# A decoder trunk on one core: the mLSTM's denominators as a 129th column of its values, and new orders of steps in the mLSTM and in the latent attention

## Chip, cores, metric

One Trainium2 chip, one core. The metric is the device time of one launch in microseconds (us); each kernel is run several times and the median is compared. TensorE (PE) does the matrix products, VectorE (DVE) and ScalarE (ACT) the elementwise work, GpSimd (POOL) small vectors, SyncE (SP) issues the loads of the weights.

## What is computed

A trunk of 4 layers on 256 tokens of width 1024, all in float32. Each layer adds half a SwiGLU (hidden width 2816), then a mixer, then half a second SwiGLU, each of an RMS-normalised input; a last RMSNorm follows. The mixers are, in order, stick-breaking attention, mLSTM, latent attention, and stick-breaking attention again. The change touches the second and the third. Of the mLSTM (8 heads, values of 128, queries and keys of 64) this matters, written for all 256 tokens at once as the kernel does it:

```python
qk, v, o_pre, gates = split(x @ w_in)                    # 1024, 1024, 1024 and 16 columns
q, k = split(silu(causal_depthwise_conv(qk, conv_w)))
s   = (q @ k.T) * weights(gates)                         # causal, per head
num = s @ v                                              # (256, 128) per head
den = sum(s, axis=-1)                                    # (256,) per head
h   = num / maximum(abs(den), exp(-m))[..., None]
out = (sigmoid(o_pre) * rmsnorm(h, head_gain)) @ w_out
```

The latent attention projects to a query latent of 384 and a key/value latent of 256 (and a rotary key of 32), RMS-normalises both latents, projects them up for 16 heads, does causal softmax attention, and projects out.

## The kernel before

**Weights.** The weights are cut into pieces of at most 128 x 2048 numbers, numbered through the whole trunk. A piece goes through a ring of three slots: SP loads it into `raw` (L453), ACT writes its high part `whi` (rounded to fp32r, times the norm's gain; L472 with a gain, L468 and L463 without), DVE writes the rest `wlo` (L491, L487, L482). PE then makes each product from three passes, high by high, low by high and high by low (`passes`, L527; `turned_block`, L1599). ACT converts piece n when PE has used piece n - 3 (`piece_used`) and the load is in; DVE follows on `hi_ready`; PE waits for `lo_ready`. The activations stand as `xT_hi` and `xT_lo`, made by transposes on PE (`fill_pe`, L558; `y_fill`, L904), a copy by ACT (`split_act`, L549) and a subtraction by DVE (`split_dve`, L553).

**Order.** There is no planner: for each mixer four functions write out the steps of PE, ACT, DVE and POOL in a fixed order, and each engine works its own list in that order. A step that waits holds all that stands behind it on its engine. Between two sublayers `last_piece` and `first_piece` (PE), `norm_act` (ACT) and `norm_dve` (DVE) do the residual, the transposes of the residual stream and its sums of squares (L602). `norm_act` works four groups: the copy of each (L549), and behind groups 2 and 3 the squares of one half of the tokens.

**mLSTM** (`ml_pe`, `ml_act`, `ml_dve`). Pieces 0 and 2 to 12 are the projections (six blocks of 512 columns, two pieces each), piece 1 the gates, 13 to 16 the output projection (`out_piece`, four groups of 6 matmuls each). Blocks 1 to 5 share PSUM banks 4 and 5, so block b + 1 starts only when `evacuate` (L935) or `output_gate` (L1358) has emptied each bank (`proj_read`). Block 0 and 1 go to `stage`, are transposed (`transposes`, L894) and convolved (`convolve`, L1426, L1428). For each of two groups of 4 heads PE writes the logarithms of the weights (`log_weights`, L1270, L1273) and the scores (L950), DVE multiplies them (`weigh`, L1440), and `numerators` makes the numerators and denominators; `outputs` (DVE, L1450) divides. Then ACT sums squares (`squares`, L1366), POOL takes the root, DVE multiplies by root and gate (`gated`, L1463), and `y_fill` / `y_split` bring the result into `xT`.

In `numerators` each head and token tile has a product of 128 columns and, with the same weights loaded again, one of a single column of ones:

```python
for n, (w, kt) in enumerate(parts):
    pe.matmul(psum[:, 6 + t, hh * P:(hh + 1) * P], w, mv[:, kt, c:c + P], ...)                        # L1295
for n, (w, kt) in enumerate(parts):
    i = pe.matmul(psum[:, 3, t * GROUP + hh:t * GROUP + hh + 1], w, ones[:, 0:1], ...)                 # L1298
```

There are 12 products of each kind for a group (one for each head of tile 0, two for each of tile 1).

**Latent attention** (`lt_pe`, `lt_act`, `lt_dve`). `latents_0`, `latents_1` make the latents; `stats` (L1581) sums their squares with 10 products by one column of ones; POOL makes the roots and a diagonal, which `spread_row` (L1587) turns into a row. `k_rope_rows` (L1592, L1593) turns the rotary key; ACT copies it (L1744) and spreads it by two DMAs (L1747), then converts piece 5. `queries(g)` (L1599) runs in two halves of 18 matmuls, into banks 4 and 7; DVE empties them (L1885, `lq_read`), and each half of `queries(1)` waits for that. Pieces 11 to 14 are the output projection. Softmax of the last two groups of heads runs beside it: `scores`, `maxima` (DVE, L1900), `exps` (ACT, L1773), `normalise` (DVE, L1912), `transposes_p` (PE, L1671), `copy_p` (ACT, L1784), `values` (PE, L1686), `y_split`.

## Time and profile before

| what | us |
|---|---|
| median of 3 runs (lowest, highest) | 1965.38 (1963.99, 1965.87) |
| the profiled execution: its time | 1964.83 |
| the profiled execution: its span | 1963.1 |
| busy in the span: PE, PE's weight load, DVE, ACT, POOL | 1937.1, 1672.2, 1367.5, 1129.2, 64.4 |

The span runs from the first to the last instruction of the profile; 1.7 us of the execution's time lie around it. All times of rows are from the span's start. The mLSTM takes some 120 us of it (685 to 808), the latent attention some 100 (1180 to 1283); the rest is the SwiGLUs and the stick-breaking attention. Matmuls overlap in the pipeline, so the duration of one is longer than what it adds: that is the distance between starts. The profile shows a float32 matmul (neither operand fp32r) as two records.

### The profile page before, as it was taken

The numbers are of one execution on the slowest core, as the hardware profiler recorded it, in microseconds if no ns is written. First come the engines' busy times: TensorE is split into PE (matmuls) and PEld (weight loads), VectorE is DVE, ScalarE is ACT, GpSimd is POOL, SyncE is SP. The second block draws the span as 40 slices with busy tenths as digits, with TensorE's granted clock in tenths as the row PEclk, the third lists the DMA queues.
The fourth block names the chain that finished last, engine by engine and source line by source line (L and its number), as shares of the span: only waits on it lengthen the run. The fifth ranks groups of instructions, "written<-read, shape, count | busy, mean of one in ns | idle before, by whom it ended". The sixth has DMA issues, their size and how long they took to land.

```text
span 1963.1 us, 29566 instructions
## 1 busy us (share of the span) xinstructions
PE 1937.1 (99%) x10788; PEld 1672.2 (85%) x10802; DVE 1367.5 (70%) x1838; ACT 1129.2 (58%) x1678; POOL 64.4 (3%) x139
## 2 busy tenths in 40 slices
PE   8999999999999999999999999999999999999998
PEld 6888988888888878888888889888888888878887
DVE  6766676767777785676777666676677766767666
ACT  6555565555655565555565555665555556556553
POOL 2000000000100000000010001000000000000000
PEclk9999999999999999999999999999999999999999
DMA  6555534556555453465555554355555555535553
GB/s 218 193 191 192 172 129 145 198 192 197 176 193 187 162 179 129 129 214 191 187 165 192 190 180 131 112 193 192 192 172 187 187 189 180 178 110 170 192 192 118
DMA packets 244095, 343.35 MB, mean 175 GB/s; under 512 B 12077, under 2 KB 196026, under 8 KB 244026
## 3 DMA queue, kind: packets, MB, share of 16 engines
q1 hardware_dynamic: 242016, 340.29, 52.2%
q10 hardware_dynamic: 2010, 2.12, 0.4%
q8 instruction: 46, 0.75, 0.2%
q14 instruction: 23, 0.19, 0.0%
HBM read 340.27 MB, written 1.05 MB: 174 GB/s over the span
## 4 chain that ended last, share of the span: by engine, by line
PE 95%; DVE 2%; ACT 1%; DMA 1%; issue 0%; SPq 0%; POOL 0%; POOLq 0%; ACTq 0%
PE psum L688 33%; PE psum L527 33%; PE psum L696 17%; PE psum L985 5%; PE psum L1599 1%; PE psum L558 1%; DVE wlo L491 1%; PE psum L950 1%; ACT whi L472 1%; PE psum L1027 1%; PE psum L1046 1%; PE psum L960 0%; PE psum L1656 0%; PE psum L1295 0%; DMA raw<-in_ffn_wi 0%
## 5 line engine op out<-in xcount | busy, mean ns | idle before, releaser
L472 ACT ACTIVATE whi<-raw,gains 128x512 fp32r<-128x512 f32 (+2 forms) x876 | 557.0, 709 | 270.1 <-PE psum L696 197.9
L688 PE MATMUL psum<-xT,whi 128*128 128x512 f32 x2816 | 679.4, 393 | 1.6 <-DVE wlo L511 1.6
L491 DVE SCALAR_TENSOR_TENSOR wlo<-raw,gains,whi 128x512 fp32r<-128x512 f32 (+2 forms) x876 | 595.8, 742 | 58.1 <-ACT whi L472 57.9
L688 PEld LDWEIGHTS psum<-xT,whi 128*128 128x128 f32 x2816 | 523.1, 189 | 110.7 <-issue 4.2
L696 PEld LDWEIGHTS psum<-xT,wlo 128*128 128x128 f32 x2816 | 349.5, 192 | 6.9
L696 PE MATMUL psum<-xT,wlo 128*128 128x256 f32 x2816 | 351.9, 283 | 0.0
L804 DVE TENSOR_TENSOR gate_in_T<-psum,low 128x512 f32<-128x512 f32 x88 | 60.8, 691 | 342.2 <-ACT low L751 341.5
L487 DVE TENSOR_TENSOR wlo<-raw,whi 128x2048 fp32r<-128x2048 f32 x100 | 228.5, 2285 | 43.8 <-ACT whi L468 43.8
L527 PE MATMUL psum<-whi,hidT_lo 128*128 128x512 f32 x640 | 249.0, 389 | 0.0
L527 PE MATMUL psum<-whi,hidT_hi 128*128 128x512 f32 x640 | 249.0, 389 | 0.0
L527 PE MATMUL psum<-wlo,hidT_hi 128*128 128x512 f32 x640 | 249.0, 389 | 0.0
L527 PE MATMUL psum<-whi,xT 128*128 128x512 f32 x704 | 230.6, 396 | 7.3 <-DVE xT L553 3.1
L468 ACT ACTIVATE whi<-raw 128x2048 fp32r<-128x2048 f32 x100 | 190.6, 1906 | 29.2 <-PE psum L696 25.3
L527 PEld LDWEIGHTS psum<-whi,xT 128*128 128x128 f32 x704 | 132.2, 188 | 37.9 <-DVE xT L553 4.0
L527 PEld LDWEIGHTS psum<-whi,hidT_hi 128*128 128x128 f32 x640 | 120.1, 188 | 25.0
L527 PEld LDWEIGHTS psum<-whi,hidT_lo 128*128 128x128 f32 x640 | 120.1, 188 | 25.0
L527 PEld LDWEIGHTS psum<-wlo,hidT_hi 128*128 128x128 f32 x640 | 120.1, 188 | 24.9
L527 PE MATMUL psum<-wlo,xT 128*128 128x512 f32 x352 | 137.2, 390 | 0.0
L766 ACT ACTIVATE hidT_hi<-hid 128x512 fp32r<-128x512 f32 x80 | 50.6, 633 | 142.6 <-PE psum L527 106.6
L759 ACT ACTIVATE silu<-gate_in_T 128x512 f32<-128x512 f32 x88 | 55.6, 632 | 106.8 <-DVE gate_in_T L806 106.7
L985 PE MATMUL psum<-xT,whi 128*128 128x256 f32 x576 | 107.3, 285 | 1.1 <-DVE mix L1145 1.1
L751 ACT ACTIVATE low<-psum 128x512 f32<-128x512 f32 x88 | 52.4, 595 | 90.2 <-PE psum L688 90.2
(231 smaller groups left out, 1565.2 us busy)
## 6 DMA issues: line engine op xcount, KB each, us to landing
raw<-in_ffn_wi SPq DMA_DIRECT2D x350, 512.0 KB, 4.6
raw<-in_ffn_wo SPq DMA_DIRECT2D x176, 512.0 KB, 4.4
raw<-in_sb_w_in SPq DMA_DIRECT2D x48, 512.0 KB, 4.4
raw<-in_ml_w_in SPq DMA_DIRECT2D x24, 512.0 KB, 4.6
raw<-in_sb_w_out SPq DMA_DIRECT2D x16, 512.0 KB, 4.2
raw<-in_ml_w_out SPq DMA_DIRECT2D x8, 512.0 KB, 4.1
raw<-in_mla_w_out SPq DMA_DIRECT2D x8, 512.0 KB, 4.3
raw<-in_mla_w_in SPq DMA_DIRECT2D x4, 512.0 KB, 4.2
```

The costliest lines, as they stand in the source:

```text
L468: act.activation(whi[:, slot, 0:w], raw[:, slot, 0:w], ACT.Copy).then_inc(hi_ready, 1)
L472: last = act.activation(whi[:, slot, r], raw[:, slot, r], ACT.Copy, scale=gain_col(p.gain + k))
L487: dve.tensor_tensor(wlo[:, slot, 0:w], raw[:, slot, 0:w], hi[:, 0:w], ALU.subtract).then_inc(lo_ready, 1)
L491: last = dve.scalar_tensor_tensor(wlo[:, slot, r], raw[:, slot, r], gain_col(p.gain + k), hi[:, r], op0=ALU.mult, op1=ALU.subtract)
L527: m = pe.matmul(dst, a, b[:, slot, cols], start=first and n == 0, stop=last and n == 2)
L688: i = pe.matmul(psum[:, 4 + blk, :], whi[:, slot, k * 2 * FC + blk * P:k * 2 * FC + (blk + 1) * P], xT[:, 4 * part + k, :, :].rearrange("p ...
L696: i = pe.matmul(psum[:, 4 + blk, 0:SEQ], wlo[:, slot, k * 2 * FC + blk * P:k * 2 * FC + (blk + 1) * P], xT_hi[:, 4 * part + k, :], start=F ...
L751: act.activation(low[:, 0, :, :], psum[:, 4:6, SEQ:2 * SEQ], ACT.Copy).then_inc(low_done, 1)
L759: act.activation(silu[:, :, :], gate_in_T[:, :, :], ACT.Silu).then_inc(silu_done, 1)
L766: act.activation(hidT(last)[0], hid[:, :, :], ACT.Copy).then_inc(hid_hi_done, 1)
L804: dve.tensor_tensor(gate_in_T[:, :, :], psum[:, 4:6, 0:SEQ], low[:, 0, :, :], ALU.add).then_inc(proj_read, 1)
L985: i = pe.matmul(dst, w[:, m % RING, c:c + P], v[:, k0 + k, :], start=k0 + k == 0 and a == 0 and blk == 0, stop=k0 + k == KD - 1 and a == 2 ...
```

## The change

Five things are done.

1. `mv` becomes (token tile, head, 129), with ones written once by POOL into column 128; `numerators` does one product of 129 columns for each pair; results stand three to a bank in banks 6, 7 and 3 (`unit`). `outputs` takes the magnitudes in two instructions and divides in four rather than two.
2. In `norm_act` ACT converts the mLSTM's piece 2 ahead of the first squares and of the copy of group 3.
3. On DVE the first half of `evac(1, stage)` goes ahead of `conv(6)`, and `evac(2, ...)` ahead of `convolve(1, (0, 1))`.
4. The first two `y_fill` of the mLSTM go ahead of piece 12, into banks 0 and 1, with their splits; the other two move to the end of `out_piece` 0 and 1.
5. In the latent attention the first half of `queries(0)` goes ahead of `stats`; piece 12 is converted ahead of `exps(2, 0)` (ACT) and of the second `y_split` (DVE); `scores(3)`, `values(2)`, `transposes_p(3)` and `values(3)` change places in the output pieces, and the third `y_split` goes behind `exps(3, 0)` and `maxima(3, 1)`.

```diff
@@ norm_act, behind norm_split(act, j, g)
+                if g == 2 and j and subs[j].kind == "ml":
+                    converts(act, convert_act, subs[j].piece0 + 2)
@@ numerators
-                            pe.matmul(psum[:, 6 + t, hh * P:(hh + 1) * P], w, mv[:, kt, c:c + P],
-                                      start=hh == 0 and n == 0, stop=n == t, skip_group_check=True)
-                        for n, (w, kt) in enumerate(parts):
-                            i = pe.matmul(psum[:, 3, t * GROUP + hh:t * GROUP + hh + 1], w, ones[:, 0:1],
-                                          start=t == 0 and hh == 0 and n == 0, stop=n == t, skip_group_check=True)
+                            i = pe.matmul(psum[:, bank, c:c + P + 1], w, mv[:, kt, GROUP * g + hh, :], start=c == 0 and n == 0,
+                                          stop=n == t, skip_group_check=True)
@@ ml_pe, end
             numerators(1)
+            y_fill(pe, s, 0, 0)
+            y_fill(pe, s, 1, 1, False)
             piece(12)
+            pe.wait_ge(tr_read, s.norm_fill0 - 4 + 2)
             pe.wait_ge(num_read, 2)
-            y_fill(pe, s, 0, 6)
-            out_piece(pe, s, 0, {1: lambda: y_fill(pe, s, 1, 7)})
-            out_piece(pe, s, 1, {1: lambda: y_fill(pe, s, 2, 6)})
-            out_piece(pe, s, 2, {1: lambda: y_fill(pe, s, 3, 7)})
+            out_piece(pe, s, 0, {3: lambda: y_fill(pe, s, 2, 6)})
+            out_piece(pe, s, 1, {3: lambda: y_fill(pe, s, 3, 7)})
+            out_piece(pe, s, 2)
@@ ml_act
-            for n in (2, 3, 4, 5):
+            for n in (3, 4, 5):
...
             conv(14)
+            y_split(act, s, 0, 0)
+            y_split(act, s, 1, 1)
             squares(1)
             output_gate(1)
-            y_split(act, s, 0, 6)
             conv(15)
-            y_split(act, s, 1, 7)
             conv(16)
@@ ml_dve
+            evac(1, stage, (0,))
             conv(6)
-            evac(1, stage)
+            evac(1, stage, (1,))
...
             conv(8)
+            evac(2, mv[:, :, 0:GROUP, 0:P])
             convolve(1, (0, 1))
-            evac(2, mv[:, :, 0:NCOL])
...
             outputs(1)
-            y_split(dve, s, 0, 6)
+            y_split(dve, s, 0, 0)
+            y_split(dve, s, 1, 1)
             gated(1)
             conv(15)
-            y_split(dve, s, 1, 7)
@@ ml_set_up (POOL)
+            pool.memset(mv[:, :, :, P:P + 1], 1.0)
@@ lt_pe
             latents_1()
+            queries(0, (0,))
             stats()
             k_rope_rows()
-            queries(0)
+            queries(0, (1,))
             spread_row()
...
-            out_piece(pe, s, 1, {0: lambda: values(2), 1: lambda: scores(3)})
-            out_piece(pe, s, 2, {1: lambda: transposes_p(3)})
-            values(3)
+            out_piece(pe, s, 1, {0: lambda: scores(3), 1: lambda: values(2)})
+            out_piece(pe, s, 2, {0: lambda: transposes_p(3), 2: lambda: values(3)})
@@ lt_act
             copy_p(1)
+            conv(12)
             exps(2, 0)
             y_split(act, s, 1, LT_AV[1])
             exps(2, 1)
-            conv(12)
             copy_p(2)
-            y_split(act, s, 2, LT_AV[2])
             conv(13)
             exps(3, 0)
+            y_split(act, s, 2, LT_AV[2])
@@ lt_dve
             maxima(2, 1)
+            conv(12)
             y_split(dve, s, 1, LT_AV[1])
             normalise(2, 0)
             normalise(2, 1)
-            conv(12)
-            y_split(dve, s, 2, LT_AV[2])
             conv(13)
             maxima(3, 0)
             maxima(3, 1)
+            y_split(dve, s, 2, LT_AV[2])
```

## Rows read from the trace of the kernel before

**Rows 1.** The page: busy time, and the groups of the weights' conversions.

```profile
PE 1937.1 (99%) x10788; PEld 1672.2 (85%) x10802; DVE 1367.5 (70%) x1838; ACT 1129.2 (58%) x1678; POOL 64.4 (3%) x139
...
L491 DVE SCALAR_TENSOR_TENSOR wlo<-raw,gains,whi 128x512 fp32r<-128x512 f32 (+2 forms) x876 | 595.8, 742 | 58.1 <-ACT whi L472 57.9
...
L487 DVE TENSOR_TENSOR wlo<-raw,whi 128x2048 fp32r<-128x2048 f32 x100 | 228.5, 2285 | 43.8 <-ACT whi L468 43.8
...
L468 ACT ACTIVATE whi<-raw 128x2048 fp32r<-128x2048 f32 x100 | 190.6, 1906 | 29.2 <-PE psum L696 25.3
```

**Rows 2.** Waits of PE: who waited for whom, us in total, times, longest.

```profile
PE psum L527 <- DVE mix L935: 1.6, 2, 1.2
```

**Rows 3.** Groups of PE's instructions by line and shape: busy us, mean ns of one.

```profile
L1295 PE MATMUL psum<-mix 128*128 128x128 f32 x48 | 8.9, 298 | 0.0
...
L1298 PE MATMUL psum<-ones,mix 128*128 128x1 f32 x48 | 6.3, 223 | 0.0
...
L1270 PE MATMUL psum<-mix 128*128 128x256 f32 x16 | 3.8, 379 | 0.0
```

**Rows 4.** Timeline of PE in the mLSTM: start, us, engine, line, instructions, idle before.

```profile
695.77 0.28 PE L1233 MATMUL psum<-xT,whi 128*16 128x256 f32 x1
697.41 0.50 PE L527 MATMUL psum<-whi,xT 128*128 128x512 f32 x1 [1.36 <-DVE wlo L491]
...
717.07 0.47 PE L527 MATMUL psum<-whi,xT 128*128 128x512 f32 x1 [1.23 <-DVE mix L935]
...
753.18 0.69 PE L1295 MATMUL psum<-mix 128*128 128x128 f32 x4
...
754.08 0.69 PE L1295 MATMUL psum<-mix 128*128 128x128 f32 x4
...
785.84 0.50 PE L527 MATMUL psum<-whi,xT 128*128 128x512 f32 x1 [1.55 <-DVE xT L553]
```

**Rows 5.** Timeline of ACT where the mLSTM begins.

```profile
687.80 1.05 ACT L602 ACTIVATE y<-h 128x1024 f32<-128x1024 f32 x1
...
690.51 0.60 ACT L549 ACTIVATE xT<-psum 128x512 fp32r<-128x512 f32 x1 [1.56 <-PE psum L558]
...
692.04 7.45 ACT L472 ACTIVATE whi<-raw,gains 128x512 fp32r<-128x512 f32 x12
```

**Rows 6.** Timeline of DVE in the mLSTM.

```profile
691.14 0.69 DVE L553 TENSOR_TENSOR xT<-psum,xT 128x512 fp32r<-128x512 f32 x1 [1.34 <-ACT xT L549]
...
716.18 1.39 DVE L935 TENSOR_SCALAR mix<-psum,rstd 128x512 f32<-128x512 f32 x2
...
772.22 2.19 DVE L1463 SCALAR_TENSOR_TENSOR y<-y,mix 128x128 f32<-128x128 f32 x8
```

**Rows 7.** Timelines of PE, ACT and DVE where the latent attention begins.

```profile
1199.71 2.39 PE L1581 MATMUL psum<-ones,mix 128*128 128x1 f32 x20 [0.47 <-ACT mix L1733]
...
1209.19 0.47 PE L1599 MATMUL psum<-sp_hi,whi 128*128 128x256 f32 x1
...
1203.28 0.38 ACT L1744 ACTIVATE mix<-psum 64x256 f32<-64x256 f32 x1 [3.63 <-PE psum L1593]
...
1207.54 0.69 DVE L1885 TENSOR_TENSOR mix<-psum,mix 128x512 f32<-128x512 f32 x1
```

**Rows 8.** Stretches there: us, busy PE, PEld, DVE, ACT, POOL with counts, clock, DMA.

```profile
1203.00:1206.40 3.40, 3.40 (x16) 3.23 (x16) 0.07 (x1) 1.53 (x3) 2.12 (x5) 0.51 0.30 69
1206.40:1210.00 3.60, 3.60 (x31) 3.55 (x31) 2.53 (x5) 0.39 (x1) 0.00 (x0) 1.00 0.78 163
```

**Rows 9.** Timelines of PE, ACT and DVE in the latent attention's output pieces.

```profile
1257.25 0.47 PE L527 MATMUL psum<-whi,xT 128*128 128x512 f32 x1 [0.99 <-DVE wlo L487]
...
1277.87 0.50 PE L527 MATMUL psum<-whi,xT 128*128 128x512 f32 x1 [1.42 <-DVE xT L553]
...
1248.43 0.56 ACT L1773 ACTIVATE mix<-psum,mix 128x256 f32<-128x256 f32 x1 [2.76 <-DVE mix L1905]
...
1251.25 0.69 DVE L553 TENSOR_TENSOR xT<-psum,xT 128x512 fp32r<-128x512 f32 x1 [1.99 <-ACT xT L549]
```

More of the change, by code:

```diff
@@ L927, in out_piece, with evacuate @@
             i.then_inc(piece_used, 1)
[L929 to L931 removed]
+        def evacuate(dve, s, b, last, dst, tiles=(0, 1)):
+            for t in tiles:
                 block_wait(dve, s, b, t, last)
[L933 to L938 removed]
+                src = psum[:, pair(b)[t], 0:math.prod(dst.shape[2:])]
+                if len(dst.shape) == 4:
+                    src = src.rearrange("p (h n) -> p h n", h=dst.shape[2])
+                dve.tensor_scalar(dst[:, t], src, rstd[:, t:t + 1], None, ALU.mult).then_inc(proj_read, 1)
         def scores_pe(pe, g, bank, k_T, q, start):
@@ L1413, in conv, with evac @@
                 converts(dve, convert_dve, s.piece0 + n)
[L1415 to L1416 removed]
+            def evac(b, dst, tiles=(0, 1)):
+                evacuate(dve, s, b, 2 * b + 2, dst, tiles)
             def convolve(part, tiles):
@@ L1606, in queries @@
                 pe.wait_ge(c_lo_done, 2)
-                for b in range(2):
+                for b in halves:
                     if g:
```

47 lines of the change are left out of this document (24 added, 23 removed).

## The prediction

> **What bounds the kernel now.** The page comes first: PE is busy for 1937.1 of 1963.1 us, no other engine for more than 70% [rows 1]. So a change can win in two ways only: fewer or shorter matmuls, or less of the 26 us in which PE stands still. The waits of PE then say what those 26 us are made of; inside the two mixers each is a wait of 0.4 to 1.6 us for one late step of DVE or ACT, as the two for `evacuate` [rows 2]. The groups by shape price the matmuls that are removed [rows 3], and the timelines show who is late and by how much [rows 4 to 7, 9]. The stretches give TensorE's granted clock [rows 8]. I do not look at the DMA queues further: every load meant here is issued two pieces ahead, and in none of these waits is a load the releaser.
>
> **Part 1, the denominators.** Each group has 12 products of one column, which stand in the profile as 24 records, 48 in all [rows 3]. One head of token tile 1 has four records of 128 columns and four of one, and takes 754.08 - 753.18 = 0.90 us [rows 4], so 0.112 us a record. That a record of one column costs as much as one of 128 is seen on `stats`: 20 records of one column take 2.39 us, 0.12 each [rows 7]; what they pay is the load of their weights. Removed: 48 x 0.112 = 5.4 us, all of it on PE and so all of it on the path, if nothing else is late.
> The Trainium skill (TensorE: Matmul & The Clock Gate, Back-to-back issue gap) has a floor of some 25 ns from start to start for small matmuls that need no new weights. By that floor the 48 records would be worth 1.2 us, not 5.4; the rows above measure 0.12 us for pairs of load and matmul, and the measurement decides.
> Added: the remaining 48 records have 129 columns. The trace has none such. Below: as 128, 0.112 us, and a little less is excluded since more is streamed. Above: the 256-column float32 records of `log_weights`, 3.8 / 16 = 0.24 us [rows 3], which would add 48 x 0.125 = 6.0 us. 129 is next to 128, so I take 0.001 us a record, +0.05 in sum, and keep +6.0 for the range. The operand rows now begin at multiples of 516 bytes; nothing in the trace shows that, and it is the reason for keeping the upper end.
> DVE's `outputs` has one more magnitude and two more divisions, of the same elements in all: some 0.4 us for each group, twice. Behind the first call stand `conv(12)` and a wait for scores that idles DVE by several us, so it costs nothing. Behind the second stand the two splits that open the output projection (part 4). POOL, busy 64.4 us in all [rows 1], does its one memset in the idle time ahead of the mLSTM. `evac` writes runs of 128 rather than of 512; its source is PSUM in both cases, at 0.69 us for each tile [rows 6], and I cost it at nothing.
>
> **Part 2, piece 2 of the mLSTM.** After the gates PE waits until 697.41 for the low part of piece 2, 1.36 us of idle [rows 4], since ACT begins its high part only at 692.04 [rows 5]. Moved ahead of the squares it begins at 687.8, takes a third of 7.45, 2.5 us, and ends at 690.4. ACT then has the squares (1.1, to 691.5) and the copy of group 3 (0.6, to 692.1), which ran at 690.51 before [rows 5]; DVE's split of it, 691.14 before, is at 692.2 to 692.9 [rows 6]. PE needs that for the gates, which it reaches at 693.1: 0.2 us to spare. DVE makes the low part by 692.9 + 4 x 0.742 less overlap, 695.6 [rows 1]; PE comes for it at 695.9, 0.3 us to spare. I take the whole 1.36. If the margins fail, by a slot or a load coming later than I think, the wait only moves in front of the gates: 0.3 is left of the gain. Next in line is the load of piece 5, which hangs on the low part of piece 2 and moves with it.
>
> **Part 3, the evacuations.** PE waits 1.23 us until 717.07, because `evac(1, stage)` stands behind `conv(6)` and runs at 716.18 [rows 4, 6]. With its first tile ahead of `conv(6)`, PE can go on at once; its second tile is wanted only by `transposes(1)`, half a piece (2.7 us) later, and is there 1.5 us before that. Gained 1.23. `evac(2)` ahead of `convolve` takes away the other wait for that line, 1.6 - 1.2 = 0.4 us [rows 2]. `conv(6)` ends 0.7 later for it, and has a whole piece of PE time to spare.
>
> **Part 4, the first transposes of the result.** PE stands idle 1.55 us until 785.84 [rows 4]: it transposes the result when piece 12 is over and waits through copy and subtraction. The first group's result is ready at 772.22 + 2.19 = 774.4, before PE ends the second numerators [rows 6], so the two fills fit there, and piece 12 (5.4 us) covers the splits. In the shortened schedule I count: numerators over at 769.8, fills to 770.8, piece 12 to 776.3; DVE `conv(14)` to 771.9, `outputs(1)` at 2.3 to 774.2, splits to 775.5. That is 0.8 us to spare, and the 1.55 goes. Who is late next: the third and fourth splits stand behind `conv(16)` and `conv(17)`, and those start when PE has used pieces 13 and 14. `y_fill(3)` finds the third split done some 0.6 us before it, and `out_piece(3)` waits some 0.1 us, as it did before.
>
> Sum of the mLSTM: 5.4 - 0.05 + 1.36 + 1.23 + 0.4 + 1.55 = 9.9 us.
>
> **Part 5a, the statistics.** PE waits 0.47 us for ACT's squares ahead of `stats` [rows 7]. Half of `queries(0)`, 18 x 0.116 = 2.1 us [rows 8], put ahead of it hides that. But `stats` and `k_rope_rows` end 2.1 - 0.47 = 1.65 us later, and a chain hangs on them: the rotary key is done when ACT copies it at 1203.28, ACT then issues two DMAs and only then converts piece 5, DVE follows and then empties `queries(0)` at 1207.54 to 1208.2 [rows 7], which `queries(1)` waits for. So that release comes 4.9 us behind the copy: at 1208.2 before, when PE came at 1209.19 [rows 7] and saw no wait, and at 1208.2 + 1.65 = 1209.9 now. PE itself will be there at about 1207.4, and stand for 2.5 us. Why did it come so late before? In 1203.00 to 1206.40 the granted clock was 0.51, the 1.2 GHz level, right after the wait and the one-column products: 16 records in 3.40 us, against 31 in 3.60 behind it [rows 8]. That cost 16 x (0.21 - 0.116) = 1.5 us, and this loss now falls into a wait. In sum the latent attention goes on at 1209.9 and not at 1209.2: **0.7 us lost**. Bounds: 0.9 gained at most if the chain were shorter than I read (PE cannot be released before its old 1208.2 plus what `stats` moved); 2.4 lost if the clock falls again in or before the new wait and slows what follows.
>
> **Part 5b, the output pieces.** PE waits 0.99 us for the low part of piece 12 and 1.42 us for the last split [rows 9]. Piece 12 on ACT (1.91 [rows 1]) fits into its idle 2.76 us ahead of `exps(2, 0)`, and on DVE (2.29 [rows 1]) into the 1.99 us ahead of the second split [rows 9]: 0.2 us over, and `normalise(2, 0)` and `transposes_p(2)` move by no more than that, with the score work behind not binding. With `values(3)` one group (1.36 us) before the end of piece 13, its copy and subtraction (0.6 + 0.7 and gaps) are just hidden. Gained: 0.99 + 1.42 = 2.4, less 0.1.
>
> **Sum.** 9.9 - 0.7 + 2.3 = 11.5 us from the profiled execution's 1964.83: **1953.3**. The median of the runs is 0.55 above that execution; I leave that in the range. The idle times of the rows leave out some 0.1 us at each wait, because a matmul's duration overlaps the next start (697.41 - 695.77 = 1.64 for an idle of 1.36 [rows 4]), so six waits may give 0.6 more.
>
> **Rivals.**
> (A) The forecast, chance 0.62.
> (B) The clock falls in the new wait ahead of `queries(1)`, or `k_rope_rows` falls into the slow stretch. For it: the one slow stretch of this trace lies just behind stall and one-column products [rows 8], and the new stall is longer than any in the mixers. Against: the waits of 1.2 to 1.6 us in the mLSTM left the clock at its upper level. Price 1.5 us again: 1954.8. Chance 0.14. The Trainium skill (TensorE: Matmul & The Clock Gate, The HAM clock gate) says that an idle array falls back to half clock and that steady work brings it back; by that, the trace agrees for the old stall, and (B) would be the outcome here.
> (C) One of the margins of 0.1 to 0.3 us in parts 2, 4 or 5b is not there, and a wait comes back in another place. Price 1 to 2 us: about 1955. Chance 0.12.
> (D) The 129th column is dear, as a second pass over the operand or as a row that begins out of line: between 0.112 and 0.24 us a record, up to +6.0: 1956 to 1959.3. For it: nothing measured. Against: the change is by one column. Chance 0.07.
> (E) The other side. The same mechanism, worse: a record of 129 columns from rows of 516 bytes costs over 0.112 + (11.5 + 3.9) / 48 = 0.43 us, so that `numerators` alone gives back more than the change brings; it decides from 0.35 us on. For that each record would take four times its present one. At 0.45: 1953.3 + 48 x 0.34 = 1969.6. Chance 0.03.
> (F) The products of one column were nearly free beside the others, so that removing them brings little: then part 1 gives 1 rather than 5.4, and 1957.7. Against it stands the even 0.112 and 0.12 of part 1. Chance 0.02.
>
> **Range and chances.** 1951.5 takes in the 0.6 of the idle times, a median like the lowest run, and a chain in 5a that costs nothing; 1957.5 takes in (B) with (C), the higher median, and the lower half of (D). About 0.2% of the time, 3.9 us, is what a measurement of this kernel tells from no change: below 1961.5 is faster. (A), (B), (C), (F) and nearly all of (D) lie there: faster 0.95, same 0.02, slower 0.03.
>
> **What would show it.** In the changed profile: L1298's records gone, those of `numerators` at 0.11 apart and 48 in number; no wait of PE for L491 behind the gates and none for `evacuate`; no wait between piece 12 and the first output piece; a new wait of about 2.5 us of PE on L1599 for DVE's L1885, the surest mark of 5a; waits for L487 and for the last split of the latent attention gone or below 0.2. The first output product of the mLSTM's piece 16 some 10 us earlier than before, that of the latent attention 11 to 12. I am wrong in the large if the distance between records of 129 columns is not 0.11 us, and in the small if a wait of over 0.5 us stands anywhere else in the two mixers.

## The result and the profile after

| | median us | lowest, highest | ratio to before, 95% interval |
|---|---|---|---|
| before, 4 runs | 1964.85 | 1963.99, 1965.87 | |
| changed, 4 runs | 1952.98 | 1952.00, 1953.34 | 0.9937 (0.9925 to 0.9949) |

The change makes the kernel faster by 11.9 us, 0.6%; the forecast was 1953.3, which is 11.5 us below the profiled execution of before and 11.55 below this median. The profiled execution of the changed kernel took 1952.87 us, with a span of 1951.1.

The busy times, from the page of the changed kernel:

```profile
PE 1929.9 (99%) x10740; PEld 1666.6 (85%) x10754; DVE 1368.4 (70%) x1844; ACT 1129.1 (58%) x1678; POOL 64.6 (3%) x140
```

PE has 48 instructions fewer than in [rows 1] and is busy for 7.2 us less; DVE has its six more (the division of `outputs` in four pieces and the magnitudes in two, for two groups). Idle time of PE in the span fell from 26.0 to 21.2 us. The waits of PE in the changed kernel (waited for, us in total, times, longest) name the larger part of these 21.2 us:

```profile
PE psum L2188 <- DMA mix<-in_ln_ffn: 5.5, 1, 5.5
PE psum L1614 <- DVE mix L1900: 2.4, 1, 2.4
...
PE psum L691 <- DVE gate_in_T L807: 0.4, 1, 0.4
PE psum L528 <- DVE xT L554: 0.2, 1, 0.2
```

The wait for the evacuation [rows 2] is not among them; those for piece 2, for the last splits and for piece 12 of the latent attention [rows 4, 9] are gone too. L1614 (`turned_block`, that is `queries(1)`) for L1900 (DVE's evacuation of `queries(0)`) is new. The first row is the start of the kernel and was there before.

To say where the time went, I take distances between two starts of PE, which no overlap of durations disturbs. Four of them are used from here on: the mLSTM (from the first transpose ahead of it to the first transpose behind it), and in the latent attention from its first transpose to the start of `queries(1)` (a), from there to the first score (b), and from there to the first transpose of the next sublayer (c).

| us | mLSTM | a | b | c |
|---|---|---|---|---|
| before | 124.08 | 31.29 | 7.67 | 65.23 |
| changed | 113.21 | 31.79 | 9.09 | 62.44 |
| difference | -10.87 | +0.50 | +1.42 | -2.79 |
| forecast | -9.9 (-10.5 with the overlaps) | +0.7 | 0 | -2.3 |

Both profiles lack one record where the first score is found: the group there has two records with 0.29 us of idle time before it, in others three records with none. So are those of `e2b`, `e5`, `e8` and `e9` below. In these six, b is 0.2 us too long and c 0.2 too short. Where kernels of both kinds are compared, I count to the record behind that group, which stands in all: so counted, b is 8.10 us before and 9.51 in the changed kernel, and c 64.80 and 62.02.

The rest of the difference lies elsewhere. The first transpose of the mLSTM comes 0.55 us earlier, ahead of all that the change touches. All of it arises in the first 20 us of the kernel, some 0.1 by the wait for the first loads and the rest in the first products behind it. This start differs from run to run: in the fourteen profiles of this study that transpose stands between 682.98 and 684.82 us, so two single runs can differ by up to 1.8 us for this alone. Behind the latent attention 0.3 us are lost, mostly in the new row above for L807. The same wait of 0.37 us stands in `e5` and `e11`, whose latent attention is as before, so the new orders did not bring it; its cause is open.

**The numerators.** Groups by shape, and PE's timeline (start, us, line, instructions), of the changed kernel:

```profile
L1303 PE MATMUL psum<-mix 128*128 128x129 f32 x48 | 5.7, 274 | 0.0
```

```profile
765.94 2.84 PE L1303 MATMUL psum<-mix 128*128 128x129 f32 x24
768.62 1.04 PE L907 MATMUL psum<-ident,y 128*128 128x128 f32 x8
...
792.62 0.50 PE L528 MATMUL psum<-whi,xT 128*128 128x512 f32 x1 [0.19 <-DVE xT L554]
```

24 records of 129 columns take 768.62 - 765.94 = 2.68 us: 0.112 each, the same as a record of 128 columns in [rows 4]. The 129th column, and rows that begin at multiples of 516 bytes, cost nothing that can be read here. Right behind stand the two early fills, and between piece 12 and the output projection there is no wait; the 0.19 at 792.62 is the fourth split, where the prediction had 0.1 and the trace of before 0.16.

**Pieces and evacuations.** ACT's and DVE's timelines of the changed kernel:

```profile
687.24 2.55 ACT L473 ACTIVATE whi<-raw,gains 128x512 fp32r<-128x512 f32 x4
```

```profile
691.35 0.69 DVE L554 TENSOR_TENSOR xT<-psum,xT 128x512 fp32r<-128x512 f32 x1 [2.11 <-ACT xT L550]
691.96 2.73 DVE L492 SCALAR_TENSOR_TENSOR wlo<-raw,gains,whi 128x512 fp32r<-128x512 f32 x4
...
710.96 0.75 DVE L939 TENSOR_SCALAR mix<-psum,rstd 128x512 f32<-128x512 f32 x1
```

Piece 2 is converted by ACT at 687.24 to 689.8 (forecast 687.8 to 690.4, in a trace that runs 0.55 later), its low part ends at 694.7, and PE comes for it at 695.3 without a wait. The first tile of `evac(1)` now stands at 710.96, ahead of the low part of piece 6.

**The latent attention.** PE's timeline where it begins, and the release chain on ACT and DVE:

```profile
1189.74 2.29 PE L1596 MATMUL psum<-ones,mix 128*128 128x1 f32 x20
...
1198.22 0.35 PE L1614 MATMUL psum<-sp_hi,whi 128*128 128x256 f32 x1 [2.39 <-DVE mix L1900]
```

```profile
1193.12 0.38 ACT L1759 ACTIVATE mix<-psum 64x256 f32<-64x256 f32 x1 [4.92 <-PE psum L1608]
1193.53 1.36 ACTq L1762 DMA_DIRECT2D mix<-mix  x2
1194.99 1.15 ACT L464 ACTIVATE whi<-raw 128x512 fp32r<-128x512 f32 x2 [1.49 <-issue]
```

```profile
1196.17 1.29 DVE L483 TENSOR_TENSOR wlo<-raw,whi 128x512 fp32r<-128x512 f32 x2 [3.89 <-ACT whi L464]
1197.39 1.28 DVE L1900 TENSOR_TENSOR mix<-psum,mix 128x512 f32<-128x512 f32 x2
```

`stats` has no wait ahead of it any more, where before it had 0.47 [rows 7]. In the order of time: the rotary key is copied at 1193.12, ACT spends 1.36 us on issuing its two DMAs, then converts piece 5 for 1.15; DVE makes the low part, and only then empties the bank that `queries(1)` wants. PE stands for 2.39 us. The stretches of the changed kernel there (us, then busy PE, PEld, DVE, ACT, POOL, then granted clock and DMA) show what follows it:

```profile
1194.00:1195.60 1.60, 1.60 (x14) 1.43 (x13) 0.00 (x0) 0.61 (x2) 1.14 (x4) 1.00 0.33 76
1195.60:1198.10 2.50, 0.23 (x2) 0.00 (x0) 1.93 (x4) 0.93 (x3) 0.00 (x0) 1.00 0.77 164
1198.10:1201.50 3.40, 3.28 (x16) 3.31 (x17) 2.04 (x4) 1.67 (x3) 0.00 (x0) 0.55 0.79 164
```

In the 3.4 us behind the wait the granted clock is 0.55, near the 1.2 GHz level, and PE does 16 products where at the upper level it did 31 in 3.6 us [rows 8]. So the slow stretch of the trace before, which lay over `queries(0)`, is still there; it has moved behind the wait, over products that the end of the kernel hangs on.

### The profile page after: what moved, and what is told of

Its sections match the earlier page's. It is cut to its first block, busy times and chain, and to the rows that moved or that the text cites. A ratio compares the mean times of both kernels' runs of the same rounds, so it can differ in the third digit from the quotient of the medians.

```text
span 1951.1 us, 29477 instructions
## 1 busy us (share of the span) xinstructions
PE 1929.9 (99%) x10740; PEld 1666.6 (85%) x10754; DVE 1368.4 (70%) x1844; ACT 1129.1 (58%) x1678; POOL 64.6 (3%) x140
## 4 chain that ended last, share of the span: by engine, by line
PE 97%; DVE 1%; ACT 1%; DMA 0%; issue 0%; SPq 0%; ACTq 0%; POOL 0%; POOLq 0%; DVEq 0%
PE psum L528 35%; PE psum L691 33%; PE psum L699 17%; PE psum L986 5%; PE psum L1614 1%; PE psum L559 1%; PE psum L951 1%; PE psum L1028 1%; PE psum L1047 1%; PE psum L961 0%; DVE wlo L492 0%; ACT whi L473 0%; PE psum L1671 0%; DMA raw<-in_ffn_wi 0%; PE psum L1701 0%; PE psum L1578 0%
## 5 line engine op out<-in xcount | busy, mean ns | idle before, releaser
L807 DVE TENSOR_TENSOR gate_in_T<-psum,low 128x512 f32<-128x512 f32 x88 | 60.9, 692 | 341.6 <-ACT low L754 340.9
```

Source lines behind the costliest of these rows:

```text
L807: dve.tensor_tensor(gate_in_T[:, :, :], psum[:, 4:6, 0:SEQ], low[:, 0, :, :], ALU.add).then_inc(proj_read, 1)
```

## The experiments

Each is the changed kernel with one edit, but for `e5_column_alone` and `e11_column_and_y`, which start from the kernel before. Here are the results of all, with distances as in the table above (the kernel of `e2` was run once more as `e2b`). The kernel before was run anew beside them, with medians of 1964.59 to 1965.46, and the ratios are to those runs. Medians that lie less than 1 us apart are therefore better compared by these ratios.

| kernel | median us (lowest, highest; runs) | ratio to before (95%) | mLSTM | a | b | c |
|---|---|---|---|---|---|---|
| e1_old_stats | 1951.19 (1951.00, 1951.39; 4) | 0.9927 (0.9911 to 0.9944) | 113.22 | 31.30 | 7.46 | 62.47 |
| e2_queries_first | 1950.04 (1948.27, 1951.75; 4) | 0.9924 (0.9908 to 0.9941) | 113.17 | 29.05 | 7.45 | 62.64 |
| e2b_again | 1948.25 (1) | | 113.18 | 29.04 | 7.67 | 62.24 |
| e3_two_products | 1957.07 (1956.28, 1957.73; 4) | 0.9956 (0.9940 to 0.9973) | 118.43 | 31.78 | 7.34 | 62.48 |
| e4_old_output | 1955.24 (1954.74, 1955.65; 4) | 0.9948 (0.9932 to 0.9965) | 113.15 | 31.78 | 8.88 | 65.44 |
| e5_column_alone | 1963.58 (1961.26, 1964.53; 10) | 0.9988 (0.9978 to 0.9997) | 121.61 | 32.85 | 7.67 | 65.23 |
| e6_old_piece2 | 1953.28 (1952.59, 1955.35; 4) | 0.9941 (0.9924 to 0.9958) | 114.85 | 31.78 | 8.77 | 62.65 |
| e7_old_evac | 1953.45 (1952.81, 1954.67; 4) | 0.9942 (0.9925 to 0.9958) | 114.86 | 31.78 | 8.71 | 62.61 |
| e8_old_y | 1956.44 (1955.79, 1957.04; 4) | 0.9956 (0.9939 to 0.9972) | 118.22 | 31.78 | 7.40 | 62.25 |
| e9_split_stats | 1948.72 (1948.15, 1948.98; 4) | 0.9917 (0.9901 to 0.9934) | 113.20 | 29.14 | 7.67 | 62.45 |
| e10_filled_wait | 1952.13 (1951.30, 1954.10; 4) | 0.9940 (0.9923 to 0.9956) | 113.18 | 31.79 | 7.34 | 62.64 |
| e11_column_and_y | 1957.80 (1956.86, 1958.56; 6) | 0.9966 (0.9953 to 0.9978) | 116.82 | 31.30 | 7.45 | 65.25 |

### The statistics as before (part 5a undone)

```diff
             latents_1()
-            queries(0, (0,))
             stats()
             k_rope_rows()
-            queries(0, (1,))
+            queries(0)
```

> The changed kernel with all of queries(0) behind stats again, as it was. Theory 1 (the chain rotary key, ACT's copy and DMA issue, piece 5, DVE's evacuation releases queries(1), and moving stats only pushed it back): PE waits 0.5 us for the squares, the wait of 2.4 us on the first queries(1) shrinks to under 0.3, the way from the sublayer's first transpose to queries(1) falls from 31.8 to 31.3 us, and from there to the first scores from 9.1 to 7.7 us, since the slow clock falls on queries(0) where the chain hides it: 1.9 us faster than the changed kernel, some 1951.1. Theory 2 (the move was worth its 0.5 us and the loss behind it is the clock alone, which falls after the one-column products in either order): the slow stretch comes all the same behind queries(1), and the time is 0.5 us longer than the changed kernel's, 1953.5.

Measured: 1951.19, that is 1.8 us faster than the changed kernel. The way from the first transpose to the record behind the first score is 39.4 us against 41.3, 1.9 less. PE's timeline and the stretches of this kernel:

```profile
1188.73 2.39 PE L1596 MATMUL psum<-ones,mix 128*128 128x1 f32 x20 [0.47 <-ACT mix L1747]
```

```profile
1192.20:1195.60 3.40, 3.40 (x20) 3.40 (x21) 0.32 (x1) 1.53 (x3) 1.96 (x5) 0.63 0.36 82
1195.60:1198.00 2.40, 2.40 (x19) 2.40 (x19) 1.57 (x3) 0.00 (x0) 0.00 (x0) 0.81 0.77 155
```

The old wait of 0.47 is back, the one ahead of `queries(1)` is gone, and the slow clock lies over `queries(0)` again. It costs little there, since PE, if it were quicker, would only wait for the release chain. So part 5a as a whole is a loss: 0.5 for the chain, 1.4 for the clock, which now falls on work that counts.

### The evacuations of `queries(0)` ahead of piece 5 on DVE

```diff
@@ lt_dve
-            conv(5)
             queries(0, 0)
             queries(0, 1)
+            conv(5)
             c_kv_scaled()
```

> The changed kernel with DVE's two evacuations of queries(0) ahead of its part of piece 5. Theory 1: the wait of 2.4 us on queries(1) goes, and with it the slow stretch of the clock behind it (1.4 us): 3.8 us faster than the changed kernel, some 1949.2; the next in line is the scaled key/value latent, done 0.3 us before PE wants it. Theory 2 (the clock falls after the one-column products anyway): the wait goes, but a slow stretch of 1.5 us stays: 2.4 us faster, 1950.6.

Measured: 1950.04, with a = 29.05, 2.7 us less than in the changed kernel, and no wait ahead of `queries(1)`. That is the whole wait, and more by the 0.3 that durations hide: the bank was late only because its evacuation stood behind the low part of piece 5. The stretch of `stats` and the rotary key in this kernel:

```profile
1192.00:1195.20 3.20, 3.20 (x23) 2.79 (x23) 0.65 (x3) 0.83 (x2) 2.69 (x5) 1.00 0.13 31
```

The clock stays at 1.00 here. But the four times fall into two pairs, 1948.47 and 1948.27 against 1951.75 and 1951.62. I ran the same kernel once more to catch a long one:

> The kernel of e2_queries_first once more, for a second trace of it. Its four times fell into two pairs, near 1948.4 and near 1951.7. If the clock explains it (theory 2), a trace with the longer time shows a slow stretch behind stats or in queries(0) that now costs its full 1.5 us, as nothing hides it; a trace with the shorter time shows none.

It took 1948.25 and its trace is like the first. With the wait gone, PE still goes through `stats` and the 32-row products of the rotary key, behind which the clock fell in `e1` and in the kernel before; that it does so in some executions of `e2` could account for the 3.3 us of the two long runs. The start, which differs by up to 1.8 us, could be a part of it. Neither long run was profiled, so this stays open.

### Two products instead of one (part 1 undone on PE alone)

```diff
@@ numerators
-                            i = pe.matmul(psum[:, bank, c:c + P + 1], w, mv[:, kt, GROUP * g + hh, :], ...)
+                            pe.matmul(psum[:, bank, c:c + P], w, mv[:, kt, GROUP * g + hh, 0:P], ...)
+                        for n, (w, kt) in enumerate(parts):
+                            i = pe.matmul(psum[:, bank, c + P:c + P + 1], w, mv[:, kt, GROUP * g + hh, P:P + 1], start=False, ...)
```

> The changed kernel, but each product of 129 columns cut into one of 128 and one of the last column, with the weights loaded twice; same banks, same outputs step. If a record of one column costs as much as one of 128 (0.11 us, the weight load), 48 more records cost 5.4 us: 1958.4. If they are nearly free (25 to 40 ns), 1.2 to 1.9 us: 1954.5. If the orders of the change hang on the shorter numerators, up to 1 us of waits is added.

Measured: the mLSTM takes 118.43 us, 5.22 more, or 0.109 for each of the 48 records; the median is 4.1 us higher. The groups by shape of this kernel:

```profile
L1303 PE MATMUL psum<-mix 128*128 128x128 f32 x48 | 8.9, 298 | 0.0
L1306 PE MATMUL psum<-mix 128*128 128x1 f32 x48 | 6.3, 223 | 0.0
```

These are the two rows of [rows 3] again, with the operand now in rows of 129 numbers: neither stride nor place changes them. In the profiled execution the slow clock fell on `queries(0)`, as this stretch shows, and most of it was hidden: counted to the record behind the first score, b is 7.99 us and not 9.51.

```profile
1199.50:1202.60 3.10, 3.10 (x19) 3.10 (x20) 0.04 (x1) 1.53 (x3) 1.95 (x5) 0.67 0.32 73
```

That is why the median could move by less than 5.22; the other three runs have no profile.

### The column alone, on the kernel before

```diff
-                            pe.matmul(psum[:, 6 + t, hh * P:(hh + 1) * P], w, mv[:, kt, c:c + P], ...)
-                        for n, (w, kt) in enumerate(parts):
-                            i = pe.matmul(psum[:, 3, t * GROUP + hh:t * GROUP + hh + 1], w, ones[:, 0:1], ...)
+                            i = pe.matmul(psum[:, bank, c:c + P + 1], w, mv[:, kt, GROUP * g + hh, :], ...)
@@ and `unit`, `outputs`, `evac`, the memset of column 128, as in the change
```

> The kernel before with the 129th column alone, all orders as before. If the removed products are worth their record price and nothing else is late: 5.4 us less in the mLSTM (its way from the first transpose to that of the next sublayer 124.1 before, 118.7 here), 1959.8 in all, and the four waits of PE in the mLSTM (1.4, 1.2, 0.4, 1.6) stand as before. Rival: the orders of before hang on the longer numerators, and the last wait grows by up to 1 us.

Measured: the mLSTM takes 121.61 us, not 118.7. It is shorter by 2.47 us only, the median by 1.3 (by 1.9 against the runs of the kernel before beside it, 1965.46). The products did not get dearer. PE's, ACT's and DVE's timelines of this kernel behind piece 12:

```profile
777.62 0.60 PE L905 MATMUL psum<-ident,y 128*128 128x128 f32 x4
781.35 0.50 PE L528 MATMUL psum<-whi,xT 128*128 128x512 f32 x1 [3.13 <-DVE xT L554]
```

```profile
776.49 0.31 ACT L1369 ACTIVATE mix<-y 128x128 f32<-128x128 f32 x1 [4.58 <-DVE y L1458]
...
778.85 1.24 ACT L1361 ACTIVATE mix<-psum,rstd 128x512 f32<-128x512 f32 x2
779.99 0.58 ACT L550 ACTIVATE xT<-psum 128x512 fp32r<-128x512 f32 x1
```

```profile
771.94 2.48 DVE L492 SCALAR_TENSOR_TENSOR wlo<-raw,gains,whi 128x1024 fp32r<-128x1024 f32 x2 [0.89 <-ACT whi L473]
```

The 1.55 us of [rows 4] have become 3.13. PE comes to the first fill earlier, but ACT's copy of it stands behind `squares(1)` (eight of 0.29 us, 776.49 to 778.85) and `output_gate(1)` (1.24 us), those behind DVE's `outputs(1)`, and that behind the low part of piece 14, which ends at 774.3. This list did not get shorter with the numerators. The stretches of this kernel show the second cost:

```profile
778.00:781.00 3.00, 0.22 (x2) 0.00 (x0) 0.40 (x1) 3.00 (x11) 1.84 (x2) 1.00 0.34 120
781.00:784.40 3.40, 3.05 (x10) 2.42 (x11) 3.40 (x10) 1.65 (x2) 0.00 (x0) 0.73 0.00 0
784.40:788.00 3.60, 3.60 (x16) 2.92 (x15) 2.08 (x3) 0.60 (x1) 0.00 (x0) 0.78 0.30 64
```

Behind the wait of 3.1 us the clock falls in part of both stretches; behind the wait of 1.55 us in the same place of the kernel before it did not. In the latent attention a is 1.56 longer than before (32.85), since the slow stretch on `queries(0)` lasted longer in this execution; so of the 2.47 us only some 0.9 are left in the trace. And 0.3 of the 2.47 do not come from the column: PE's first wait for an evacuation is 0.85 us here and was 1.23, for a reason that the section on pieces 2 and 3 shows.

### The first fills as before (part 4 undone), and parts 1 and 4 together

```diff
@@ e8, ml_pe (ACT's and DVE's lists go back likewise)
             numerators(1)
-            y_fill(pe, s, 0, 0)
-            y_fill(pe, s, 1, 1, False)
             piece(12)
+            y_fill(pe, s, 0, 6)
...
@@ e11: the kernel before, with the column as in e5 and the lists of part 4 as in the change
```

> The changed kernel with the first two transposes of the mLSTM's result behind piece 12 again. The wait of 1.55 us comes back between the first of them and the output projection; 1.7 us by the distance of starts: 1954.7. Rival: numerators end 2.7 us sooner relative to the splits than before, so that DVE's squares and gates are late as well and more than 2 us come back.

> The kernel before with the 129th column and the early transposes of the result, nothing else. The column alone brought only 2.5 us in the mLSTM, since the wait behind piece 12 grew from 1.55 to 3.13 us and the clock fell behind it. Here that wait cannot stand: the mLSTM's way from the first transpose to the next sublayer's falls by 5.3 + 1.7 = 7.0 from 124.1 to 117.1 us, four and a half more than the column alone, and the total is 1958.3. If the growth of the wait had another cause, part of it comes back in another place, and the way is 118 or more.

Measured: without part 4 the mLSTM takes 118.22 us, 5.01 more than in the changed kernel, where the forecast had priced part 4 at 1.55 and the expectation above at 1.7. PE's timeline and the stretches of that kernel:

```profile
778.38 0.50 PE L528 MATMUL psum<-whi,xT 128*128 128x512 f32 x1 [3.12 <-DVE xT L554]
```

```profile
778.00:781.40 3.40, 3.02 (x10) 2.42 (x11) 3.40 (x10) 1.68 (x2) 0.00 (x0) 0.75 0.00 0
781.40:785.00 3.60, 3.60 (x16) 2.91 (x15) 2.11 (x3) 0.60 (x1) 0.00 (x0) 0.76 0.28 64
```

It is the wait of 3.1 us and the clock behind it, as in `e5`. Its median is only 3.5 us above the changed kernel; in the profiled execution the clock fell on `queries(0)` in the latent attention (b is 7.40 against 9.09, the record missing in both). Parts 1 and 4 on the kernel before bring 124.08 - 116.82 = 7.26 us. Their forecast terms were 5.4 and 1.55, in sum 6.9 with the 129th column; the rest, 0.3, has the size of the overlap at one wait. So these two terms are right together and wrong one by one: part 1 alone is worth 2.5, part 4 in its presence 4.8 (7.26 - 2.47) on the kernel before and 5.0 on the changed one.

### Piece 2, and the evacuations (parts 2 and 3 undone)

```diff
@@ e6: norm_act and ml_act
-                if g == 2 and j and subs[j].kind == "ml":
-                    converts(act, convert_act, subs[j].piece0 + 2)
-            for n in (3, 4, 5):
+            for n in (2, 3, 4, 5):
@@ e7: ml_dve
-            evac(1, stage, (0,))
             conv(6)
-            evac(1, stage, (1,))
+            evac(1, stage)
...
-            evac(2, mv[:, :, 0:GROUP, 0:P])
             convolve(1, (0, 1))
+            evac(2, mv[:, :, 0:GROUP, 0:P])
```

> The changed kernel with the conversion of the mLSTM's piece 2 behind the squares again. The wait of 1.4 us for its low part comes back, 1.5 us by the distance of starts, and the steps behind it move along: the mLSTM's way 113.2 becomes 114.7, the total 1954.4. Rival: the load of piece 5, which hangs on it, comes late and adds a wait of its own.

> The changed kernel with the two evacuations behind conv(6) and behind convolve again. The waits of 1.23 and 0.37 us come back, by the distance of starts 1.4 and 0.4; since piece 2 is earlier than in the kernel before, the first may be larger by up to 0.3 us. The mLSTM's way 113.2 becomes 115.0 to 115.3, the total 1954.9.

PE's timelines, first of the kernel with the old piece 2, then of the one with the old evacuations:

```profile
697.82 0.50 PE L528 MATMUL psum<-whi,xT 128*128 128x512 f32 x1 [1.38 <-DVE wlo L492]
```

```profile
714.73 0.47 PE L528 MATMUL psum<-whi,xT 128*128 128x512 f32 x1 [0.76 <-DVE mix L939]
```

Each wait is back in its place (beside the 0.76 also the one of 0.37 at 730.87), and each mLSTM is longer by 1.64 and 1.65 us. Part 2 is thus worth 1.64 (forecast 1.36) and part 3 1.65 (1.63). But the first wait for an evacuation is 0.76 us, where it was 1.23 before. ACT's timelines, of the kernel before and of the one with the old evacuations, show what set it:

```profile
703.70 2.56 ACT L472 ACTIVATE whi<-raw,gains 128x512 fp32r<-128x512 f32 x4 [4.20 <-DMA raw<-in_ml_w_in]
```

```profile
701.37 2.56 ACT L473 ACTIVATE whi<-raw,gains 128x512 fp32r<-128x512 f32 x4 [2.89 <-DMA raw<-in_ml_w_in]
```

This is piece 5, whose conversion starts when its load is in: 19.5 us behind the mLSTM's first transpose before, 17.4 here. DVE makes its low part next, and everything up to the evacuation follows without a gap in DVE's list. So with piece 2 early this load comes 2.1 us earlier, PE only 1.6, and the wait is shorter by the difference. In `e5` and `e11` the load came at 19.2 and 19.4, and the wait was 0.85 and 1.10.

Beside this the medians rise by only 0.30 and 0.47 us (by the ratios, 0.8 and 1.0). In both kernels the profiled execution is the longest of the four, by 1.7 and 1.0 us, and without it the others lie around 1953. Part of that is the start: the first transpose of the mLSTM comes 0.95 and 0.33 us later in these two profiles than in that of the changed kernel. An execution in which the clock does not fall behind the wait of `queries(1)` would be shorter too, but I have no profile of one. The distances decide for what a part saves; what the median moved by is not settled for these two.

### The output pieces as before (part 5b undone)

```diff
@@ lt_pe (ACT's and DVE's lists go back likewise)
-            out_piece(pe, s, 1, {0: lambda: scores(3), 1: lambda: values(2)})
-            out_piece(pe, s, 2, {0: lambda: transposes_p(3), 2: lambda: values(3)})
+            out_piece(pe, s, 1, {0: lambda: values(2), 1: lambda: scores(3)})
+            out_piece(pe, s, 2, {1: lambda: transposes_p(3)})
+            values(3)
```

> The changed kernel with the order of the latent attention's output pieces, conversions and splits as before. The two waits of PE, 1.0 for piece 12 and 1.4 us for the last split, come back as they were: 2.4 by the idle times, 2.8 by the distance between the first scores and the first transpose of the next sublayer (62.4 now, 65.2 before): 1955.8. Rival: DVE's and ACT's queues have moved so that only one of the two comes back: 1954.2.

The waits of PE in this kernel:

```profile
PE psum L1614 <- DVE mix L1901: 2.4, 1, 2.4
...
PE psum L528 <- DVE xT L554: 1.6, 2, 1.4
...
PE psum L528 <- DVE wlo L488: 1.0, 1, 1.0
```

Both waits of [rows 9] are back; counted from the record behind the first score, c is 64.79, 2.8 us more than in the changed kernel, and the median 2.3 more. The forecast had 2.4 - 0.1 for it. The difference is again what durations hide at two waits, and the 0.1 that I took off was not lost.

### Is it the wait that lets the clock fall?

```diff
@@ lt_pe
             spread_row()
+            pe.wait_ge(table_read, 2)
+            for _ in range(18):
+                pe.matmul(psum[:, 0, 0:SEQ], c_hi[:, 0, 0:P], c_hi[:, 0, :], start=True, stop=True)
             queries(1)
```

> The changed kernel with 18 products of 256 columns into a bank that is free, put ahead of queries(1), where PE waits 2.4 us; they compute nothing that is used. If it is the long wait that lets the clock fall behind it, 2.1 us of added work cost nothing and bring 1.4 us: from queries(1) to the first scores 7.6 us and not 9.1, no stretch below the upper level behind queries(1), 1951.5 in all. If the one-column products bring the fall, it comes as before and the time is the changed kernel's 1953.0 or a little more.

PE's timeline and the stretches of this kernel:

```profile
1195.44 2.49 PE L1717 MATMUL psum<-sp_hi 128*128 128x256 f32 x18
1198.18 0.36 PE L1614 MATMUL psum<-sp_hi,whi 128*128 128x256 f32 x1 [0.24 <-DVE mix L1903]
```

```profile
1195.50:1198.10 2.60, 2.44 (x20) 2.20 (x18) 1.96 (x4) 0.99 (x3) 0.00 (x0) 1.00 0.78 165
1198.10:1201.50 3.40, 3.32 (x28) 3.35 (x29) 2.70 (x6) 1.68 (x3) 0.00 (x0) 1.00 0.79 168
```

`queries(1)` starts as late as before (a = 31.79), held by the same release, but 18 products whose result nobody reads fill the time ahead of it. The clock stays at 1.00, 28 products run in the 3.4 us that held 16, and b, counted to the record behind the first score, falls from 9.51 to 7.99 us. In this profile filling the time kept the clock up, so it is the engine's standing still that made it fall in this place; the 1.5 us are its price. This rests on one profile against four with the wait (the changed kernel, `e4`, `e6`, `e7`), in each of which the clock fell behind it. The profiled run took 1951.30, the other three 1952.42, 1951.84 and 1954.10: the median is only 0.85 below the changed kernel, and by the ratios to the kernel before (0.9940 against 0.9937) nothing is gained. The times of whole runs thus do not show the effect; only the trace does.

### A version that avoids both

```diff
@@ lt_pe, with DVE's list as in e2
+                    if c:                                   # in latents_1, behind the rotary half
+                        pe.wait_ge(c_hi_done, 2)
+                        stat_products(lambda k: k < 4)      # 16 of the 20 records
...
             latents_1()
-            queries(0, (0,))
-            stats()
             k_rope_rows()
-            queries(0, (1,))
+            stats()                                         # the products for k == 4 alone
+            queries(0)
```

> The changed kernel with DVE's evacuations of queries(0) ahead of piece 5, and with stats cut in two: the 8 products whose squares are ready stand between the two halves of the second latent piece, the rotary key next, which covers the wait for the last squares, then the last 2 products and all of queries(0). Theory 1 (a release chain from the rotary key) and theory 2 (the clock falls behind a stretch of one-column products) agree that no wait is left: 29.1 us from the first transpose to queries(1). They differ in the clock: if one-column products and the 32-row products in one piece bring the fall, it should be gone here in every execution, and the runs should lie together at 1949, where e2_queries_first spread over 1948.3 to 1951.8.

PE's timeline and the stretches of this kernel:

```profile
1184.06 1.84 PE L1590 MATMUL psum<-ones,mix 128*128 128x1 f32 x16
...
1188.79 0.69 PE L1615 MATMUL psum<-mix 32*128 32x256 f32 x2
...
1189.85 0.61 PE L1590 MATMUL psum<-ones,mix 128*128 128x1 f32 x4
```

```profile
1184.00:1188.00 4.00, 4.00 (x37) 4.00 (x36) 2.41 (x3) 0.00 (x0) 0.00 (x0) 1.00 0.13 36
1188.00:1192.00 4.00, 4.00 (x30) 3.47 (x29) 0.23 (x2) 0.94 (x3) 1.10 (x2) 1.00 0.49 152
1192.00:1196.00 4.00, 4.00 (x34) 3.95 (x33) 1.85 (x3) 1.36 (x3) 1.58 (x4) 1.00 0.78 162
```

Most of the one-column products are done while the second half of the latents is still to come, the rotary key goes ahead of the last four, and there is neither a wait nor an unbroken row of 20 small products. The clock is 1.00 throughout. The median is 1948.72, 4.3 us below the changed kernel (3.9 by the ratios) and 16 below the one before, the four runs within 0.8 us of each other: the lowest median of several runs. Its fast runs are no faster than those of `e2` (1948.3); what it adds is that no run near 1951.7 came. Four runs are few for that, and whether breaking up the row did it is not shown.

## Why the prediction was right

**Part 1, the numerators: right in its sum, under a condition that only part 4 met.** Each of the 48 one-column records cost 0.109 (`e3`), 0.112 was forecast, and the 129th column costs nothing. But "all of it on PE and so all of it on the path, if nothing else is late" passes over the point: without part 4 something is late at once. Alone, more than half of the 5.4 us went into a longer wait behind piece 12 and into the clock (`e5`). Rivals D, E and F are excluded: the products were neither dear with 129 columns nor nearly free with one. The floor of 25 ns of the Trainium skill (TensorE: Matmul & The Clock Gate, Back-to-back issue gap), named in the prediction, would have made these records worth 1.2 us; `e3` says 5.22. The prediction had it for products that need no new weights, and every one of these records loads its own.

**Parts 2 and 3: right.** 1.64 and 1.65 us against 1.36 and 1.63. Both margins of part 2 held: the low part of piece 2 is there 0.6 us before PE comes (forecast 0.3). The term of part 2 was too small by what the idle column leaves out, as the prediction had said of it. That of part 3 is right partly by luck: the idle column leaves out 0.5 us at its two waits, and the first wait was 0.5 us shorter once piece 2 was early. The prediction had said that in none of these waits a load is the releaser. That is so one step back, but the chain of DVE and ACT ahead of the evacuation began with the load of piece 5.

**Part 4: right in place, too small for what it does.** The step "the 1.55 goes" took the wait from the trace of before, and that wait was to grow with part 1. Worked out on the shortened schedule, as the margins were, it would have been 3.1 us with a slow clock behind it. The error does not show in the total, since part 1 was credited with what belongs to part 4: 7.26 measured for both. The spare time before the first output product was 0.8 us, as forecast (DVE's splits end at 774.1; piece 12 begins at 769.4 and takes 5.6, so PE comes at 775.0).

**Part 5a: the mechanism right, its price off by the clock.** The new wait was forecast at 2.5 us and measured 2.39, at the instruction and for the release that the prediction named; with its chain from the copy of the rotary key to the evacuation, 5.1 us from 1193.12 to 1198.2, where 4.9 was read. The cost up to `queries(1)` was 0.5 us (0.7 forecast). What failed is the end of its sum, "this loss now falls into a wait". The slow clock of [rows 8] did leave `queries(0)`, but did not vanish into the wait: it began behind it and cost 1.4 us more (b = 9.09 against 7.67). That is rival B, at about the price of 1.5 that it had been given: the forecast counted it as the less likely case (0.14). I had held against it that the waits of 1.2 to 1.6 us in the mLSTM left the clock alone; the new wait was longer than any of them, and `e5` and `e8` show that one of 3.1 us in the mLSTM does have a slow stretch behind it. The rule of the Trainium skill (TensorE: Matmul & The Clock Gate, The HAM clock gate), that an idle array falls back to half clock, led to the right outcome here, and `e10` agrees: with the idle time filled, the clock stayed up. The prediction had also counted the old slow stretch as a case of it, with a stall of 0.47 us ahead. `e3` and `e8` speak against that: there the same stretch comes with no wait ahead of it.

**Part 5b: right.** 2.8 us against 2.3; the two waits went, and nothing came in their place.

**The total.** The loss by the clock (1.4) was made up by terms that were too small: 1.0 in the mLSTM (10.87 against 9.9) and 0.5 in the output pieces, of which 0.6 had been foreseen as overlap. The earlier start of 0.55 us is luck, and 0.3 were lost behind the latent attention. So the 0.3 us between forecast and median are smaller than most of the errors inside it: that they cancel is luck too, though each part went the way that was forecast. Rival C did not come: the largest new wait beside that of `queries(1)` in the two mixers is 0.19 us. The marks given for the profile held: the end of the mLSTM comes 11.4 us earlier (0.55 of it the start), that of the latent attention 12.3 (11.8 without the start; 11 to 12 forecast).

## What to carry to other kernels

When a bottleneck engine gets shorter, reprice every wait behind the shortened stretch on the new schedule before adding up: a wait read from the old trace grows by up to what the engine gains, and parts of a change that touch one wait can only be priced together. A wait on TensorE costs more than its length once it is long (here 2.4 us and 3.1 us, with about 1.5 us lost behind it), so a move that ends in such a wait should be priced with the clock behind it. A slow stretch costs little while a later wait would take up the time anyway; a move that shifts it onto the path pays for it in full. Follow the chain of a wait back by more than one step: here it began with a load. In an order written out by hand, an evacuation that another engine waits for goes ahead of a conversion that nobody wants yet; here that one exchange of two lines took away a wait of 2.4 us.

## What the runs showed of the hardware

The clock fell in two situations. One is a long wait: behind 2.38 to 2.39 us (changed, `e4`, `e6`, `e7`) and behind 3.1 us (`e5`, `e8`), not behind 1.55 us or less in the mLSTM. The other has hardly any wait in it: in `e1`, as in [rows 8], the 20 records of one column (2.39 us) and the few 32-row products of the rotary key come in a row, with 0.47 us of idle ahead, and the clock was at 0.63 in the 3.4 us from 1192.20 although PE was busy throughout. With the 0.47 us ahead of the row, the clock fell in all four profiles (before, `e1`, `e5`, `e11`). With no wait ahead of it, it fell in two (`e3`, `e8`) and stayed up through the row in seven (changed, `e2`, `e2b`, `e4`, `e6`, `e7`, `e10`). In `e9`, with the row broken up, there is no slow stretch, which after those seven proves little. So where the slow stretch falls differs between kernels whose latent attention is the same up to there, and one profile is not enough to price it.

A float32 product that loads its 128 x 128 weights anew costs 0.11 us a record whether 1 column (`e3`: 0.109), 128 ([rows 4]: 0.112) or 129 (changed: 0.112) are streamed.
